# Key and value weights behind the modulation loads, bias rows stored head by head, row sums ahead of their splits, and an own count for one weight quarter

## The reference

```python
shift, scale, gate = jnp.split(c @ ada_w + ada_b, 3, axis=-1)
h = rmsnorm(x, norm_g) * (1 + scale[:, None, :]) + shift[:, None, :]
q, kc, vc, ksl, vsl, kw, vw, gts, hc, bc, cc, z = split_proj(h @ w_in)   # 1024 x 6960
k_cmp, v_cmp = compress(kc, pe_k, w1_k, w2_k), compress(vc, pe_v, w1_v, w2_v)
# attention per head: compressed blocks, 16 selected blocks, a window of 512,
# each with the relative position bias tab[bucket(distance)]; summed with sigmoid gates
u = cc * hc
y_conv = bc * short_conv(u_pad, conv_w)
o = concatenate([o_attn * silu(z_a), y_conv * silu(z_c)]) @ w_out
y = rmsnorm(x + gate * o, final_g)
```

## Time and profile before

| | |
|---|---|
| median of three runs | 1536.29 us (1535.63 to 1536.37) |
| the profiled execution | 1532.23 us, its span 1530.4 us |
| PE busy | 1433.0 us, 94% of the span |
| DVE, ACT, POOL busy | 964.0, 704.4, 234.7 us |
| granted TensorE clock, mean | 0.979 |
| share of the last chain | PE 80%, DVE 7%, DMA 5%, ACT 3%, issue 3% |
| stage 1 / projection / compression start | 0 / 147.6 / 662.7 us |

### The profile page before, as it was taken

One profiled execution on the slowest core, in us unless ns is written; L12 is line 12 of the kernel. 1 busy time (PEld: TensorE's weight loads), 2 busy tenths in 40 slices (PEclk: granted clock), 3 DMA queues, 4 the chain that ended last, 5 costly groups with the idle time before them and its releaser, 6 DMA issues.

```text
span 1530.4 us, 27904 instructions
## 1 busy us (share of the span) xinstructions
PE 1433.0 (94%) x10526; PEld 1236.4 (81%) x10526; DVE 964.0 (63%) x2312; ACT 704.4 (46%) x1546; POOL 234.7 (15%) x441
## 2 busy tenths in 40 slices
PE   5987998999999999969989999999999999999998
PEld 2876998999999999957767777777777766788886
DVE  2643768787787887848666666667567654653226
ACT  2421232423323223226567777777777765631111
POOL 1100010101101011031021242232222131000000
PEclk9998999999999999989999999999999999999999
DMA  9376123423333334297321141121121129963231
GB/s 345 99 137 126 28 84 90 117 60 96 86 75 105 78 90 112 62 316 237 111 91 43 29 108 56 43 70 47 33 57 30 30 74 357 265 207 98 82 98 35
DMA packets 169669, 164.76 MB, mean 108 GB/s; under 512 B 53644, under 2 KB 150028, under 8 KB 164160
## 3 DMA queue, kind: packets, MB, share of 16 engines
q1 hardware_dynamic: 153904, 94.11, 22.6%
q0 software_dynamic: 15632, 68.87, 14.9%
HBM read 131.27 MB, written 35.83 MB: 109 GB/s over the span
## 4 chain that ended last, share of the span: by engine, by line
PE 80%; DVE 7%; DMA 5%; ACT 3%; issue 3%; SPq 1%; DVEq 0%; POOL 0%; ACTq 0%
PE PS L1258 26%; PE PS L1619 11%; PE PS L1425 8%; PE PS L1390 7%; PE PS L1369 5%; PE PS L1307 4%; PE PS L1370 3%; PE PS L1472 2%; PE PS L1214 1%; DMA gw<-in_ada_w 1%; PE PS L1215 1%; PE PS L1216 1%; DMA adaw<-in_ada_w 1%; PE PS L1576 1%; DMA wr<-in_w_in 1%
## 5 line engine op out<-in xcount | busy, mean ns | idle before, releaser
L1258 PE MATMUL PS<-bo,wsl 128*128 128x264 f32 x4104 | 504.5, 286 | 11.1 <-DVE qp L2186 5.8
L1258 PEld LDWEIGHTS PS<-bo,wsl 128*128 128x128 f32 x4104 | 503.6, 190 | 12.2 <-DVE qp L2186 6.0
L1882 ACT ACTIVATE pr<-PS,nm 128x640 f32<-128x640 f32 (+7 forms) x256 | 181.0, 708 | 45.2 <-DVE nm L2392 42.6
L1715 ACT ACTIVATE wsl<-wsum 128x512 fp32r<-128x512 f32 x105 | 65.6, 630 | 231.9 <-DVE wsum L2107 231.9
L1905 ACT ACTIVATE ptt<-PS 128x512 f32<-128x512 f32 x264 | 149.6, 601 | 41.6 <-PE PS L1390 41.4
L1390 PE MATMUL PS<-ident,pr 128*128 128x128 f32 x1056 | 147.2, 274 | 0.0
L1425 PE MATMUL PS<-ptt,kvt 128*64 128x256 f32 x1056 | 136.7, 390 | 0.0
L1390 PEld LDWEIGHTS PS<-ident,pr 128*128 128x128 f32 x1056 | 122.4, 141 | 8.9 <-ACT ptt L1905 0.4
L1425 PEld LDWEIGHTS PS<-ptt,kvt 128*64 128x64 f32 x1056 | 66.9, 136 | 41.2 <-issue 16.5
L2392 DVE CUSTOM_DVE_ANT_0 PS<-PS,near,nm 128x256 f32<-128x256 f32 x192 | 94.7, 493 | 6.8
L2391 DVE TENSOR_REDUCE nm<-PS 128x1 f32<-128x128 f32 (+5 forms) x128 | 70.5, 551 | 39.2 <-PE PS L1370 38.7
(11 more groups left out here) (358 smaller groups left out, 2403.2 us busy)
## 6 DMA issues: line engine op xcount, KB each, us to landing
wr<-in_w_in SPq DMA_DIRECT2D x32, 512.0 KB, 5.6
adaw<-in_ada_w SPq DMA_DIRECT2D x8, 1024.0 KB, 9.5
wr<-in_w_in SPq DMA_DIRECT2D x32, 256.0 KB, 4.3
q_stacked<-qp POOLq DMA_DIRECT2D x64, 128.0 KB, 2.7
qb<-q_stacked SPq DMA_DIRECT2D x32, 256.0 KB, 3.1
mr<-mixed SPq DMA_DIRECT2D x16, 512.0 KB, 3.9
mixed<-yy POOLq DMA_DIRECT2D x16, 264.0 KB
xb<-in_x_prompt POOLq DMA_DIRECT2D x8, 512.0 KB, 4.7
```

The costliest lines, as they stand in the source:

```text
L1258: ins = pe.matmul(PS[:, 2 * q + c, 0:H // 2], w[:, x, kk, :], b[:, y, kk, c * H // 2:(c + 1) * H // 2], start=(first and kk == 0 and x == ...
L1882: act.activation(pr[r][:, h, 0:k], score_cols(b0, w), ACT.Exp, scale=-1.0, bias=nm[:, r, h:h + 1], accum_out=rsum[:, r, h:h + 1]).then_inc ...
```

## The change

Four things are changed, and what they need.

1. SP loads `wkr[0]` behind the eight `adaw` loads instead of ahead of them, and `wkr[1]` counts on another semaphore (`wk1_ld`). ACT makes the high part of `wkr[0]` behind its copies of the modulation, that of `wkr[1]` behind the first two tiles' high parts; DVE makes the low part of `wkr[0]` behind the modulated first prompt tile.
2. The bias rows lie in free partitions of another tile (`kvs[64:80]`), and each head's row has a store of its own, 192 KB, in blocks 4 to 19 (`store_bias`, ahead of product 4 of the block in POOL's program). The single store and the waits of ACT and POOL for it are gone.
3. Block 0 multiplies in another order: the two products with `O12` first. PE waits for the key evacuations ahead of the second product and for `ada_ev` ahead of the fourth. The pieces of the operand sums have two tables, `ADDED` and `SPLIT`: a sum stands ahead of the low part of the piece before it, the last eight sums are all made by block 2, product 2, in `ts`, `eg`, `er` and in place in `qp`, and their low parts follow in products 3 to 6. All sums take two operations. `query_high` waits for 16 low parts.
4. The first quarter of `w1` counts on the weight semaphore of the projection. PE waits for it alone ahead of step 0, and for the other three ahead of step 8.

```diff
-            sp.dma_start(wkr[0][:, :, :], w3[:, :, O_KV:O_KV + KV0]).then_inc(wk_ld, 16)
             for k in range(KC):
                 if k >= 4:
                     sp.wait_ge(ada_mm, k - 3)
                 sp.dma_start(adaw[k][:, :], ada3[:, k, 0:2 * D]).then_inc(adaw_ld[k % 4], 16)
-            sp.dma_start(wkr[1][:, :, :], w3[:, :, O_KV + KV0:O_H]).then_inc(wk_ld, 16)
+            sp.dma_start(wkr[0][:, :, :], w3[:, :, O_KV:O_KV + KV0]).then_inc(wk_ld, 16)
+            sp.dma_start(wkr[1][:, :, :], w3[:, :, O_KV + KV0:O_H]).then_inc(wk1_ld, 16)
...
-            po.wait_ge(tb_ev, 1)
-            rv = rows[:, :]
-            po.dma_start(rowd, bass.AP(rv.tensor, rv.offset, [list(rv.ap[0]), [0, P], [1, XW]])).then_inc(row_st, 16)
+            def store_bias(h):
+
+                rv = rows[h:h + 1, :]
+                po.dma_start(rowd[h:h + 1], bass.AP(rv.tensor, rv.offset, [list(rv.ap[0]), [0, P], [1, XW]])).then_inc(row_st, 16)
...
+                    if i == 4 and 4 <= n < 4 + NH:
+                        store_bias(n - 4)
...
-            pe.wait_ge(kv_ev, 2 * NTT)
             pe.wait_ge(h_ev, NTT)
...
-            pe.wait_ge(ada_ev, 8)
             for n in range(NBLK):
                 for i in range(products(n)):
                     if plain(n):
-                        k, op, out = PLAIN[i]
+                        k, op, out = PLAIN[(2, 3, 0, 1)[i] if n == 0 and i < 4 else i]
+                        if n == 0 and i == 1:
+                            pe.wait_ge(kv_ev, 2 * NTT)
+                        if n == 0 and i == 3:
+                            pe.wait_ge(ada_ev, 8)
...
-            pe.wait_ge(xp_ld[2], 64)
+            pe.wait_ge(wr_ld, raw_landed(NBLK - 1) + 16)
             for m in range(32):
+                if m == 8:
+                    pe.wait_ge(xp_ld[2], 48)
...
-                    if (n, i) in PIECES:
-                        x = PIECES[n, i]
-                        if x:
-                            op_low(x - 1)
-                        if x == 12:
-                            whole(O11)
+                    for x in ADDED.get((n, i), ()):
                         op_add(x)
-                    if n == NPLAIN and i == 2:
-                        op_low(19)
+                    for x in SPLIT.get((n, i), ()):
+                        op_low(x)
+                    if n == 1 and i == 6:
+                        whole(O11)
```

More of the change, by code:

```diff
@@ L140, in build @@
         kvt = sb("kvt", [P, NTT - 1, KVW - KOFF], cx=cV)
+        rows = kvs[64:64 + NH, 0:XW]
         krow = kvt[0:33, 7, 0:XW]
@@ L583, in summed_at, with sum_ready, op_sum32 @@
             return tuple(m for m in prepared_at(n, i) if is_sum(m))
[L585 to L590, removed]
+        PIECE = [(s_, k) for s_ in range(5) for k in range(HK)]
+        ADDED = {(0, 0): (0,), (0, 1): (1,), (0, 2): (2,), (0, 3): (3,), (0, 4): (4,), (0, 5): (5,), (0, 6): (6,), (0, 7): (7,),
+                 (1, 0): (8,), (1, 1): (9,), (1, 4): (10,), (1, 5): (11,), (1, 7): (16, 17), (2, 0): (18, 19), (2, 1): (12, 13), (2, 2): (14, 15)}
+        SPLIT = {(0, 1): (0,), (0, 2): (1,), (0, 3): (2,), (0, 4): (3,), (0, 5): (4,), (0, 6): (5,), (0, 7): (6,), (1, 0): (7,),
+                 (1, 1): (8,), (1, 4): (9,), (1, 5): (10,), (1, 6): (11,), (2, 3): (12, 13), (2, 4): (14, 15), (2, 5): (16, 17), (2, 6): (18, 19)}
+        def sum_ready(x):
+            return x + 1 if x < 12 else x + 5 if x < 16 else x - 3
+        def op_sum32(x):
+            if x < 12:
+                return (er if x % 2 else ts[0])[:, :]
+            return f32(qp[:, x - 12, :]) if x < 16 else (ts[1], eg, ts[0], er)[x - 16][:, :]
         ACT_EV = {(0, True): "cc1 cc0", (1, True): "zt1 zt0", (2, True): "za1 qh1 za0 qh0",
@@ L1717, in op_high @@
             def op_high(x):
[L1719 to L1724, removed]
+                s_, k = PIECE[x]
+                act.wait_ge(op_sum, sum_ready(x))
+                if x >= 12:
+                    act.wait_ge(*made(2, 3 if x >= 16 else 1))
+                act.activation(bo[SUMS[s_][0]][:, 0, k, :], op_sum32(x), ACT.Copy).then_inc(op_hi, 1)
             def copied_out(dst, src, func=ACT.Copy, scale=1.0):
@@ L1738, in query_high @@
                 else:
-                    act.wait_ge(op_sum, 16 if half else 18)
+                    act.wait_ge(op_lo, 16)
                 copied_out(halves(qp[:, 2 * half, :]), src, ACT.Copy, -0.125)
@@ L1825, in _ @@
                         high(m)
-                    if (n, i) in PIECES:
-                        op_high(PIECES[n, i])
+                    for x in ((ADDED if n < 2 else SPLIT).get((n, i if n < 2 else i + 1), ())):
+                        if (x < 12) == (n < 2):
+                            op_high(x)
                 if n == 4:
@@ L2124, in op_add @@
                 dst, a, b, op = SUMS[s_]
-                t = op_scratch(x)
-                if x >= 2:
+                t, kept = op_sum32(x), f32(qp[:, k, :])
+                if 2 <= x < 12:
                     dve.wait_ge(op_lo, x - 1)
-                if x < 18:
-                    dve.wait_ge(op_kept, 1 if x < 12 else 2)
-                    first_, second = (f32(bo[a][:, 0, k, :]), f32(qp[:, k, :])) if s_ < 4 else (f32(qp[:, k, :]), f32(bo[b][:, 0, k, :]))
-                    link(dve.tensor_tensor(t[0][:, :], first_, second, op))
-                    dve.tensor_tensor(t[0][:, :], t[0][:, :], f32(bo[a if s_ < 4 else b][:, 1, k, :]), ALU.add).then_inc(op_sum, 1)
-                else:
-                    dve.tensor_tensor(t[0][:, :], f32(bo[a][:, 0, k, :]), f32(bo[b][:, 0, k, :]), op)
-                    link(dve.tensor_tensor(t[1][:, :], f32(bo[a][:, 1, k, :]), f32(bo[b][:, 1, k, :]), op))
-                    dve.tensor_tensor(t[0][:, :], t[0][:, :], t[1][:, :], ALU.add).then_inc(op_sum, 1)
+                if x >= 16:
+                    dve.wait_ge(op_lo, 12)
+                dve.wait_ge(op_kept, 1 if x < 12 else 2)
+                if 12 <= x < 16:
+                    dve.wait_ge(op_sum, 16)
+                own, first_, second = (b, kept, f32(bo[b][:, 0, k, :])) if s_ == 4 else (a, f32(bo[a][:, 0, k, :]), kept)
+                link(dve.tensor_tensor(t, first_, second, op))
+                dve.tensor_tensor(t, t, f32(bo[own][:, 1, k, :]), ALU.add).then_inc(op_sum, 1)
             def op_low(x):
-                (s_, k), t = PIECE[x], op_scratch(x)
+                s_, k = PIECE[x]
                 dst = bo[SUMS[s_][0]]
-                dve.wait_ge(op_sum, x + 1)
+                dve.wait_ge(op_sum, sum_ready(x))
                 dve.wait_ge(op_hi, 1 + x + 1)
-                dve.tensor_tensor(dst[:, 1, k, :], t[0][:, :], f32(dst[:, 0, k, :]), ALU.subtract).then_inc(op_lo, 1)
+                dve.tensor_tensor(dst[:, 1, k, :], op_sum32(x), f32(dst[:, 0, k, :]), ALU.subtract).then_inc(op_lo, 1)
             def conv_inputs(n):
```

36 lines of the change are left out of this document (18 added, 18 removed).

## The result

The changed kernel takes **1575.12 us** (median of four runs, 1573.23 to 1578.96) against 1535.96 us before: ratio 1.0259, 95% interval 1.0236 to 1.0282, so 36 to 43 us slower. Forecast was 1506. The profiled execution spans 1571.3 us, 40.9 more than before.

A forecast was written before the change was run, and what follows sets the result against it. PE, busy in 94% of the span, bounds the kernel, so only its waits give time back. Terms 0.8 + 13.7 + 5.8 + 8.6 + 4.0 - 3.0 = 29.9 us gained give 1506 us for the median, range 1496 to 1518.

The forecast's parts named there:

- Term 6: Blocks 4 to 19: the sixteen small bias-row stores make weight loads late, 3.0 us lost (0 to 11).
- The slower rival: Blocks 4 to 19: one-partition stores at half rate or less hold every block's weight load; 1551 us, chance 0.02.
- Term 2: Gate products before the projection: without the 3 MB bias store, the gate-load wait and its clock cost go; 13.7 us gained.
- Terms 3 and 4: Projection start and block 3: PE's waits for gate sums and a query's low part go; 5.8 and 8.6 us gained.
- Term 5: Compression: first weight quarter counted alone, step 4 then waits for the tail store; 4.0 us gained (1 to 6).
- Term 1: Sample products: first key/value weight tile loaded behind the modulation loads; 0.8 us gained (1 lost to 1.9 gained).
- step 1: Same claim as Term 1: sample products start earlier, 0.8 us gained; a later start than 40.2 us would refute it.

The follow-up runs named there:

- rows_alone: Kernel before with only the second part: bias rows in partitions 64 to 79, sixteen one-head stores; 1598.86 us (one run).
- all_heads: Changed kernel, but each of the sixteen stores writes 8 copies of all 16 heads, read from sixteen partitions; 1498.96 us, ratio 0.9759.
- spread_heads: Changed kernel, but each store writes 32 copies of four heads lying in partitions four apart; 1505.14 us, ratio 0.9803.
- block_start: Changed kernel with its one-head stores issued at the start of blocks 5 to 20 instead of in product 4; 1513.09 us (one run).
- heads_tails: all_heads with the two convolution tails' stores issued ahead of the second gather and of the wait for the query stores; 1494.24 us, ratio 0.9723.
- order_alone: Kernel before with only the block-0 order of products and the order of sums and splits; 1521.67 us, ratio 0.9923.
- quarter_alone: Kernel before with only the own count for the first compression weight quarter; 1527.89 us, ratio 0.9954.
- old_store: Changed kernel with its second part undone: one 3 MB store at its old place before the gate loads; 1517.5 us, ratio 0.9888.
- four_heads: Changed kernel, but each store writes 32 copies of four neighbouring heads, read from four partitions; 1580.86 us (one run).

## Why the prediction was wrong, step by step

**Term 6, the small stores, failed: 3.0 us was put down, 74.0 us were measured.** Its first sentence held the error: "Each carries a sixteenth of the old one: 35.3/16 = 2.2 us of the DMA engines." The bytes are a sixteenth, but the old store read four groups of four partitions at once and each new one reads one partition. A store's time was divided by its bytes where it should have been worked out from where it reads. Everything behind that line followed: "Against it: each is over in 2 us", "A pair adds 0 to 4.4 us" (its second store landed up to 16.4 us after its issue), and a bound of 11 us that was no bound. The ways in which lateness travels were right: load, VectorE's sum, PE. Of the five pairs behind the query stores, four made the four longest stops (7.1 to 9.1 us) and one made 4.1.

**The slower rival had the mechanism, with too small a price and too small a chance.** It named one-partition stores at half rate or less, and 4.5 us of lateness as its point. At 43 and 33 GB/s against 101, less than half the rate was measured, and the eleven stops were 1.9 to 9.1 us long. It gave 3 us a store and 1551; the runs show 74.0 / 16 = 4.6 us a store and 1575, since stores in pairs add up, and each stop pays the clock again. It got a chance of 0.02, "against it: the blocks without a pair have room" (the single stores made stops of 1.9 to 4.7 us), although no row of the trace showed a one-partition store at all. An operation that no row shows should have had the wide range; 35.3 us for sixteen partitions bounds one partition from below (2.2 us, if all share one limit) and from above (if each partition gives its own share alone: 35.3 us).

**Term 2 held.** The gate wait is gone. In rows_alone, which has part 2 and not part 1, T0 lies at 133.43 - 4.11 = 129.3 for 143.5: 14.2 us, forecast 13.7. In the changed kernel it lies at 130.4: 13.1 us for terms 1 and 2 together, which were forecast at 14.5. In all_heads, spread_heads, block_start and heads_tails it lies at 128.8 to 130.7.

**Terms 3 and 4 held.** 14.4 us were forecast and 14.4 lie between the medians of order_alone and the kernel before; in its trace T0 to the projection's end is 499.6 us for 515.5, 15.9 less. With an interval of 8 to 16 us, that forecast and medians meet to the tenth is luck. VectorE is in time in block 3, as worked out from its waits: in order_alone it waits 8.8 us for ScalarE in the 79 us from T0 on (9 were forecast), and the low part of the first block's queries is done at 220.24, 75.1 us behind T0 (76 were forecast).

**Term 5: mechanism right, size right in its stage.** Step 4 does wait, 3.8 us in the changed kernel and 4.1 in quarter_alone (5 to 8 were expected), and VectorE's wait there ends with the tails' store, as said. I took the store's landing as 677; in quarter_alone VectorE went on at 677.07. The lower clock came as well: 0.50 from 678 to 684. PE starts the product of step 4 at 678.46 for 685.01 before, 6.6 us ahead, and at 701.09 for 704.74 it is only 3.7 us ahead, 0.5 of which it already had at the projection's end. So the stage gained 3.2 us, forecast 4.0 (1 to 6), and the clock took 2.9, forecast 2.3. Yet the medians differ by 8.2 us (5 to 9), and the two traces by 6.7. Of these, 3.0 us lie behind the compression of the keys, in work that this part doesn't touch. From there to the end the thirteen traces take 799 to 808 us, in no order that fits an edit; why quarter_alone is at the low end of that was not found.

**Term 1 failed by its own sign, and its price stays open.** The prediction says that "a first sample product later than 40.2 us" makes step 1 wrong. The sample products began at 41.04 instead of 40.17, which would be a loss of 0.9 us, inside its bounds of 1 lost to 1.9 gained. The wait there, 8.8 us, ends when a key/value weight has landed. In the eight traces with the part they begin at 40.7 to 41.1, in the five without it at 38.4 to 40.4. T0 in the changed kernel is 1.1 us later than in rows_alone, which lacks the part. But undoing the part on heads_tails cost 0.6 points of the ratio (intervals 0.9698 to 0.9749 and 0.9762 to 0.9803), which is 4 to 14 us. Its traces show 4.8 us, 2.8 before the projection and 2.2 in a wait far behind it that this part doesn't touch. Against that, old_store, which has terms 1, 3, 4 and 5, gained 17.8 us between the medians, and terms 3 and 4 alone 14.4 and term 5 alone 8.2, which leaves no gain for term 1. No cause for the difference was found.

Without term 6 the sum was 32.9 us; all_heads, which has the other five and stores that are nearly free, gained 36.3 between the medians and 30.3 between the two profiled executions. The whole miss is the one term.

## What to carry to other kernels

Price a DMA by the partitions that it reads or writes at once, not by its bytes alone: a store that is cut into pieces should be cut so that each piece still touches all groups of four partitions, here by copies and not by heads. A transfer that is slow for that reason books every DMA engine that it is spread over while it moves little, so look for a DMA share near 1 beside a low rate, and for the load that is queued behind it. And where a change brings an operation that the trace doesn't show, its bounds must come from what could limit it, not from one division.

## What the runs showed of the hardware

- Four neighbouring partitions have one way out of SBUF for DMA, of 25 to 30 GB/s. Packets of 4.6 KB took 0.18 us with one engine to a group (spread_heads; 26 GB/s, which may be that engine's own limit), 0.74 us when four engines shared a group (the kernel before and four_heads), 2.4 to 2.5 us when sixteen did (the changed kernel and block_start).
- Mean DMA share does not tell the harm. Over 200 to 640 us the POOL queue's packets took this share in the changed kernel and in four_heads, in this order, and both lost the same time:

```profile
q0 software_dynamic: 5552, 16.98, 29.3%
```

```profile
q0 software_dynamic: 7527, 16.76, 19.0%
```

  In the first all engines are slow for a short time, in the second a few are held for as long, and a load that is spread over all of them would wait for the last one, which is an argument and was not measured.
- A stop of PE costs more than it lasts: 19.6 us of longer work at a lower clock (0.94 for 0.99) on top of eleven stops, 1.8 us each (rows_alone).
